# Prompt attention with the values as the stationary operand and its outputs turned back

## The reference, cut to what matters

```python
o_cmp, p_cmp = attend_dense(q, k_cmp, v_cmp, dist_c, dist_c >= 0, rel_bias)
o_sel = sel_attend(q, qpos, idx, kb, vb, rel_bias)
o_win = win_attend_prompt(q, k_win, v_win, rel_bias)
g = jax.nn.sigmoid(ngate.astype(F32)).reshape(B, T, 3, NSA_KV, NSA_REP)[..., None]
o_c = (g[:, :, 0] * o_cmp + g[:, :, 1] * o_sel + g[:, :, 2] * o_win)
```

## Time and profile before

| | |
|---|---|
| three runs | 3067.50, 3078.32, 3078.89 us |
| median | 3078.32 us |
| the profiled execution | 3082.61 us |
| its span in the trace | 3081.1 us, mean granted clock 0.944 |
| prompt attention in it, first score to last output | from 1620 to 1966 us |
| busy over the span | PE 91%, weight loads (PEld) 83%, DVE 43%, ACT 27%, POOL 13% |

### The profile page before, as it was taken

The page is one execution under the profiler, slowest core; times in us unless marked ns, Lnnn a source line. Parts: engine busy times, 40 slices in busy tenths (PEclk is TensorE's granted clock), DMA queues, the critical chain, the costliest instruction groups (busy, mean ns, idle before and its releaser), DMA issues. The chain is left out here.

```text
span 3081.1 us, 46606 instructions
## 1 busy us (share of the span) xinstructions
PE 2809.5 (91%) x17082; PEld 2572.7 (83%) x17082; DVE 1310.7 (43%) x3005; ACT 836.7 (27%) x1558; POOL 412.9 (13%) x562
## 2 busy tenths in 40 slices
PE   6999997999995799857958999899999999999998
PEld 6888997988985667753638888689989999999998
DVE  7555421443452476424526665454453332133321
ACT  4221111112011344423425665432232221011110
POOL 2121001222221233217720000000000000000000
PEclk8999998999997799978978998999999999999999
DMA  3222123223223577547731112323311113211132
GB/s 128 96 72 67 59 98 113 85 85 107 78 85 113 148 212 223 158 121 214 212 100 57 49 49 69 129 78 121 121 70 41 48 43 120 83 41 48 41 105 86
DMA packets 194205, 305.98 MB, mean 99 GB/s; under 512 B 41423, under 2 KB 147086, under 8 KB 191942
## 3 DMA queue, kind: packets, MB, share of 16 engines
q1 hardware_dynamic: 163650, 218.50, 22.5%
q0 software_dynamic: 20400, 63.59, 5.9%
q10 hardware_dynamic: 10004, 21.99, 2.1%
HBM read 238.73 MB, written 78.24 MB: 103 GB/s over the span
## 5 line engine op out<-in xcount | busy, mean ns | idle before, releaser
L2580 PE MATMUL tr_ps<-tr_act_in_r,tr_w_hi 128*128 128x364 f32 (+1 forms) x2496 | 486.2, 330 | 0.0
L2580 PEld LDWEIGHTS tr_ps<-tr_act_in_r,tr_w_hi 128*128 128x128 f32 x2496 | 428.0, 189 | 0.0
L2580 PE MATMUL tr_ps<-tr_wide_r,tr_w_hi 128*128 128x364 f32 (+1 forms) x1632 | 317.1, 330 | 0.0
L2580 PE MATMUL tr_ps<-tr_act_in_r,tr_w_r 128*128 128x364 f32 (+1 forms) x1248 | 277.7, 331 | 14.2 <-DVE tr_act_in_r L2821 7.1
L2580 PEld LDWEIGHTS tr_ps<-tr_wide_r,tr_w_hi 128*128 128x128 f32 x1632 | 278.6, 188 | 0.0
L2580 PEld LDWEIGHTS tr_ps<-tr_act_in_r,tr_w_r 128*128 128x128 f32 x1248 | 218.7, 189 | 15.5 <-issue 15.5
L63 PE MATMUL hg_ps<-tokens_hi,hg_gw_r 128*128 128x364 f32 (+1 forms) x576 | 195.7, 340 | 27.5 <-POOL hg_gw_r L2180 18.7
L65 PE MATMUL hg_ps<-tokens_hi,hg_gw_hi 128*128 128x364 f32 (+1 forms) x576 | 191.7, 333 | 0.0
L64 PE MATMUL hg_ps<-tokens_r,hg_gw_hi 128*128 128x364 f32 (+1 forms) x576 | 191.4, 332 | 0.0
L2580 PE MATMUL tr_ps<-tr_wide_r,tr_w_r 128*128 128x364 f32 (+1 forms) x816 | 180.6, 330 | 3.3 <-DVE tr_wide_r L2776 3.3
L2672 ACT ACTIVATE tr_w_hi<-tr_w 128x1024 fp32r<-128x1024 f32 (+2 forms) x76 | 88.7, 1167 | 310.0 <-DMA tr_w<-w_down_in 184.7
(11 more groups left out here) (510 smaller groups left out, 5271.3 us busy)
## 6 DMA issues: line engine op xcount, KB each, us to landing
cc_pages<-cache_in SPq DMA_DIRECT2D x256, 128.0 KB, 3.4
tr_w<-w_gate_up_in SPq DMA_DIRECT2D x44, 512.0 KB, 3.5
sa_v_pages<-cache_in POOLq DMA_DIRECT2D x256, 64.0 KB, 2.4
sa_k_pages<-cache_in SPq DMA_DIRECT2D x256, 64.0 KB, 2.3
proj_feat<-hg_g_stage POOLq DMA_DIRECT2D x24, 544.0 KB
tr_act_in<-proj_feat SPq DMA_DIRECT2D x24, 544.0 KB, 5.6
hg_gw<-w_gates_in SPq DMA_DIRECT2D x24, 512.0 KB, 3.4
tr_w<-w_down_in SPq DMA_DIRECT2D x16, 704.0 KB, 4.0
```

The lines of the kernel that those rows point to most:

```text
L2580: last = pe.matmul(ps[:, 3 * bs + c, 0:z - a], wp, xp[:, k, a:z], start=(k == 0 and n == 0), stop=(k == len(tiles) - 1 and n == 2))
```

## The change

`values` makes the values the stationary operand (64 columns) and the turned probabilities the moving one (128 columns). The selected product is written to partitions 0 to 63 of bank 7, the window product to partitions 64 to 127, key tile by key tile in turn; the compressed one is computed twice, once for each half, into the next 128 columns. All products of a tile wait for the tile's last copy. The outputs now have the head's dimensions on the partitions, so DVE copies 256 columns of bank 7 to SBUF (`take_outputs`) and PE turns them back by two transposes into the other half of bank 7 (`turn_back`): one of 128x128 and one of 64 rows. `turn_back(n - 2)` stands between the selected and the window scores of tile n. DVE's order becomes: copy and outputs of tile n - 2, then the bias of tile n. `cols` gets a third set of columns, since sums live one tile longer.

```diff
-        cols = sb("cols", [P, 2, 24])
+        cols = sb("cols", [P, 3, 24])
+        o_t = sb("o_t", [P, 2, 2 * P])
...
                 last.then_inc(S["sel_mm"], 1)
+                if n >= 2:
+                    turn_back(n - 2)
                 w0 = win_first(i) * P
...
-                def copied(x):
-
-                    if x % 4 == 0:
-                        pe.wait_ge(S["pt_copied"], base_chunk[n] + x // 4 + 1)
-
+                w0 = win_first(i)
+                heads = slice(g * HD, (g + 1) * HD)
+                sel, win = ps[0:HD, 7, 0:P], ps[HD:P, 7, 0:P]
+
+                pe.wait_ge(S["pt_copied"], base_chunk[n + 1])
                 for k in range(i + 1):
-                    copied(k)
-                    pe.matmul(ps[:, 7, 0:HD], p_all(n, k, P), v_all[:, 0, k, g * HD:(g + 1) * HD], start=(k == 0), stop=(k == i))
-                w0 = win_first(i)
-                for k in range(w0, i + 1):
-                    copied(i + 1 + k - w0)
-                    pe.matmul(ps[:, 7, HD:2 * HD], p_all(n, i + 1 + k - w0, P), v_all[:, 1, k, g * HD:(g + 1) * HD], start=(k == w0), stop=(k == i))
-                copied(len(tiles) - 1)
-                pe.matmul(ps[:, 7, 2 * HD:3 * HD], p_all(n, len(tiles) - 1, NB), vc[:, g * HD:(g + 1) * HD], start=True, stop=True).then_inc(S["o_mm"], 1)
+                    pe.matmul(sel, v_all[:, 0, k, heads], p_all(n, k, P), start=(k == 0), stop=(k == i))
+                    if w0 + k <= i:
+                        pe.matmul(win, v_all[:, 1, w0 + k, heads], p_all(n, i + 1 + k, P), start=(k == 0), stop=(w0 + k == i))
+                for x in range(2):
+                    last = pe.matmul(ps[x * HD:(x + 1) * HD, 7, P:2 * P], vc[:, heads], p_all(n, len(tiles) - 1, NB), start=True, stop=True)
+                last.then_inc(S["o_mm"], 1)
+
+            def turn_back(n):
+
+                pe.wait_ge(S["o_read"], n + 1)
+                pe.transpose(ps[:, 7, 2 * P:3 * P], o_t[:, n % 2, 0:P], ident[:])
+                pe.transpose(ps[:, 7, 3 * P:3 * P + HD], o_t[0:HD, n % 2, P:2 * P], ident[0:HD, 0:HD]).then_inc(S["o_back"], 1)
...
+            turn_back(NH * NT - 2)
             values(NH * NT - 1)
+            turn_back(NH * NT - 1)
...
+            def take_outputs(n):
+                dve.wait_ge(S["exp_done"], 3 * (n + 1))
+                dve.wait_ge(S["o_mm"], n + 1)
+                if n >= 2:
+                    dve.wait_ge(S["o_back"], n - 1)
+                dve.tensor_copy(o_t[:, n % 2], ps[:, 7, 0:2 * P]).then_inc(S["o_read"], 1)
+
             def finish(n):
...
-                dve.wait_ge(S["o_mm"], n + 1)
+                dve.wait_ge(S["o_back"], n + 1)
...
                 for n in range(h * NT, (h + 1) * NT):
+                    if n >= 2:
+                        take_outputs(n - 2)
+                        finish(n - 2)
                     bias_and_max(n)
-                    if n >= 1:
-                        finish(n - 1)
                     if n % NT == NT // 2 + 1 and h + 1 < NH:
                         queries_lo(h + 1)
-            finish(NH * NT - 1)
+            for n in range(NH * NT - 2, NH * NT):
+                take_outputs(n)
+                finish(n)
```

More of the change, by code:

```diff
@@ L1776, in prompt_attention_stage @@
         S = {n: new_sem("pa_" + n) for n in
-             ("keys_in values_in gates_in gate_exp sel_mm win_mm sel_neg win_neg exp_done pt_tr pt_copied o_mm o_read tile_set passed anyc k_zero k_hi k_split q_hi q_split").split()}
+             ("keys_in values_in gates_in gate_exp sel_mm win_mm sel_neg win_neg exp_done pt_tr pt_copied o_mm o_read o_back tile_set passed anyc k_zero k_hi k_split q_hi q_split").split()}
         out_stored = [new_sem(f"pa_out_stored{n}") for n in range(2)]
@@ L1958, in _ @@
                     nw = hi - win_first(i) * P
-                    c = cols[:, n % 2]
+                    c = cols[:, n % 3]
                     if n >= 1:
@@ L2028, in bias_and_max @@
                 dve.tensor_scalar(c[:, 1:3], c[:, 18:20], -1.0, None, ALU.mult).then_inc(S["win_neg"], 1)
+            def take_outputs(n):
[4 more added lines that the diff above has]
+                dve.tensor_copy(o_t[:, n % 2], ps[:, 7, 0:2 * P]).then_inc(S["o_read"], 1)
             def finish(n):
                 h, i = at(n)
-                c = cols[:, n % 2]
-                dve.wait_ge(S["exp_done"], 3 * (n + 1))
+                c = cols[:, n % 3]
                 dve.reciprocal(c[:, 12:15], c[:, 4:7])
@@ L2042, in finish @@
                 o = out[:, h % 2, i]
-                dve.tensor_scalar(o, ps[:, 7, 0:HD], c[:, 13:14], None, ALU.mult)
+                dve.tensor_scalar(o, ps[:, 7, 2 * P:2 * P + HD], c[:, 13:14], None, ALU.mult)
                 dve.drain()
-                dve.scalar_tensor_tensor(out=o, in0=ps[:, 7, HD:2 * HD], scalar=c[:, 14:15], in1=o, op0=ALU.mult, op1=ALU.add)
+                dve.scalar_tensor_tensor(out=o, in0=ps[:, 7, 2 * P + HD:3 * P], scalar=c[:, 14:15], in1=o, op0=ALU.mult, op1=ALU.add)
                 dve.drain()
-                dve.scalar_tensor_tensor(out=o, in0=ps[:, 7, 2 * HD:3 * HD], scalar=c[:, 12:13], in1=o, op0=ALU.mult, op1=ALU.add).then_inc(S["tile_set"], 1)
+                dve.scalar_tensor_tensor(out=o, in0=ps[:, 7, 3 * P:3 * P + HD], scalar=c[:, 12:13], in1=o, op0=ALU.mult, op1=ALU.add).then_inc(S["tile_set"], 1)
             for h in range(NH):
                 for n in range(h * NT, (h + 1) * NT):
+                    if n >= 2:
+                        take_outputs(n - 2)
+                        finish(n - 2)
                     bias_and_max(n)
-                    if n >= 1:
-                        finish(n - 1)
                     if n % NT == NT // 2 + 1 and h + 1 < NH:
                         queries_lo(h + 1)
-            finish(NH * NT - 1)
+            for n in range(NH * NT - 2, NH * NT):
+                take_outputs(n)
+                finish(n)
 LB_FLOOR = 1e-30
```

## The result

The changed kernel takes 3101.91 us, the median of five runs (3095.88 to 3108.52), against 3078.32 before: 23.6 us or 0.8% slower; the ratio of the means is 1.0083 with a 95% interval of 1.0060 to 1.0106. The forecast was 3120, the range 3085 to 3150. The profiled execution took 3101.91 us, its span is 3100.4, 19.3 more than the 3081.1 of the profiled one before.

What follows compares the result with a forecast made beforehand. PE, 91% busy, was taken to bound the kernel, the stage counting in full. +4.1 us a head, 29 for seven, +1 first head, +1 end, +11 clock make +42 on the profiled 3082.6; against the median, 3120 us, range 3085 to 3150.

Steps and rivals of the forecast that it cites:

- (a): Selected and window products on PE: paired halves at 0.055 us an instruction instead of 0.111, gaining 6.75 us a head.
- rival that the halves do not run side by side: Products on PE: at 0.110 us each they gain nothing, 12.6 us a head lost, 3180 us; chance 0.02.
- (b): Before each tile's products: PE waits for the last copy of probabilities, not the first, losing 5.46 us a head.
- rival that PE's saved time counts: Products and copies: the copy wait costs nothing, so -2.75 us a head, 3056 us; chance 0.08.
- (c): Between selected and window scores: two more turning transposes on PE cost 0.5 us a step, 4.0 a head.
- (d): Before the turning transposes: PE waits for DVE's copy of the products, mainly in small steps, 1.2 us a head.
- rival of a nearly free turning: Turning transposes at 0.2 us a step and half the wait for DVE's copy: +7 us, 3085 us; chance 0.14.
- (e): DVE's loop in step 1, the shortest: copy and turning lengthen it past PE's own way, 0.2 us a head.
- The first head: Stage's first head, partly at the low clock, where the products gain more: forecast at +1 us.
- The end: Behind the stage's last tile, copy and turning stand bare: forecast at +1 us.
- (f): Granted clock at step 1, longer with less work: falls in four heads instead of two, +11 us.
- rival of a fall in every head: Granted clock: falls in five more heads at 7.0 us each, +66 us in all, 3144 us; chance 0.15.

Runs made afterwards that it cites:

- wait alone: Kernel before with its old products, each tile's products waiting for the tile's last copy, nothing else changed; 3133.94 us, 1.0192.
- 128 rows: Changed kernel with the second turning transpose over all 128 rows and columns instead of 64 rows; 3080.35 us, 1.0002 of the kernel before.
- second record: A kernel profiled again unchanged: the kernel before took 3078.18 us, the changed kernel 3104.87 us.
- no turning: Changed kernel without DVE's copy and both turning transposes, outputs reading unturned products; 3069.14 us, 0.9978 of the kernel before.
- both repairs: Changed kernel with products in chunk order, each chunk awaiting its own copy, and the compressed product in its old form; 3042.10 us, 0.9873 of before.
- old compressed form: Changed kernel with compressed probabilities stationary again, one turning transpose and a DVE copy of 128 columns; 3073.13 us, 0.9984 of the kernel before.
- one half after the other: Changed kernel with all selected products of a tile first, then all window products; 3136.18 us, 1.0199 of the kernel before.
- order of chunks: Changed kernel with selected and window tiles laid out in turn, each chunk's products waiting only for its own copy; 3085.61 us, 1.0011 of before.

## Why the prediction was right, and where not

**(a) Products**, -6.75 forecast, -6.69 measured. The spacing in the sample attention's rows carried over. The rival that the halves do not run side by side fell.

**(b) The wait for the last copy**, 5.46 forecast, 5.42 in the changed kernel and 5.5 with the wait alone. The list of waits has 55 us, inside the forecast 50 to 80. The rival that PE's saved time counts fell with it.

**(c) and (d) Turning**, 5.2 together, 5.10 measured. From the first turning transpose to the window scores PE takes 0.26 + 0.20 = 0.46 us in steps 0 to 3 and 0.40 to 0.43 in the others, in place of 0.5: 3.5 a head, which leaves 1.6 for the wait. The one part was 0.5 too high and the other 0.4 too low; that they cancel is luck. The rival of a nearly free turning (0.2 a step) describes the variant with 128 rows better than the change: its two transposes take 0.14 to 0.19.

**(e)** 0.2 forecast, 0.21 measured, 0.14 of it in step 1; that step is 3.73, forecast 3.6 to 3.8.

So seven heads at full clock cost 28.5 us (six differences that add up to 13.6, 10.9 of the lost clock of before added to them, and 4.0 for the last head), forecast 29.

**The first head**, forecast +1, measured 52.30 - 46.77 = +5.5: it loses the 4.0 of any head, and 1.5 more (52.30 - 44.31 = 8.0 over a head at full clock, before 6.5), with a low clock at its beginning that lasted 36.1 us of it instead of 25.5. Why it lasted longer is open; in the second record of the kernel before it was 18.3 us, in that of the changed one 35.7.

**The end**, forecast +1: the last head and what stands behind it grew by 6.1, 4.0 of which is the head, so 2.1.

**(f) The clock** is the step that failed. It said that four heads would fall instead of two, because step 1 gets longer with less work in it: +11. In the profiled execution no head fell, which gave 10.9 us back. The second record, with two falls costing 3.6 + 1.3 = 4.9 us, makes the gain smaller but not the forecast right: before, the falls in heads 2 to 8 cost 10.9 and, in its second record, 6.9 + 3.9 + 3.8 = 14.6. Nor do the executions without a trace: the changed kernel's five have a higher mean clock than the 48 of before (0.948 against 0.944 to 0.945). The premise had come true: PE idles 0.86 to 1.15 us in every step of head 4, 0 to 0.72 before, so that more idle time stands beside fewer falls. In step 1 its share is the same, 0.93 of 3.73 us against 0.72 of 2.90. The place was right: all falls of all records of heads 2 to 8, but for those of the wait alone, begin 8.5 to 10.9 us after a head's start, in step 1 or at the beginning of step 2. The reason was not. Falls in heads 2 to 8 (not counting the end of the stage, where every record has one), by the length of steps 0 and 1 of head 4, one number for each record:

| kernel | steps 0 and 1, us | falls |
|---|---|---|
| before | 5.62, 2.90 | 2, 3 |
| wait alone | 6.79, 2.90 | 6, in 5 heads |
| no turning | 5.64, 3.19 | 1 |
| both repairs | 5.12, 3.38 | 0 |
| old compressed form | 5.98, 3.39 | 0 |
| 128 rows | 6.24, 3.64 | 1, of 3.4 us |
| changed | 6.53, 3.73 | 0, 2 |
| one half after the other | 7.24, 3.74 | 1 |
| order of chunks | 5.55, 3.74 | 5, 5 |

A step 1 of 3.74 us stands beside five falls and beside none. What decides is left open, and with one or two records for each kernel the rows can only rule out a strict order: neither the length of step 1, nor the wait (most falls with the old products, few with the new), nor the form of the products (the chunk order has the new form and five falls) orders the rows. The rival of a fall in every head is wrong all the same, and so is the one that transposes hold no clock.

The sum: 28.5 + 5.5 + 2.1 - 10.9 = +25.2 in the stage. It started 8.4 us earlier than in the profile of before (1611.8 against 1620.2); in the other records it starts between 1609.9 and 1619.7, the kernel before at 1617.3, so this is the stages ahead, which the change does not touch. Behind the stage 2.5 us were added. 25.2 - 8.4 + 2.5 = 19.3, the spans' difference; the profiled execution of before lay 4.3 over its median, which makes the 23.6 of the medians. The forecast's sum was 42, so it was 18 too high: 21.9 too much for the clock, 5.9 for what lies outside the stage and 0.5 for seven heads, less 4.5 and 1.1 too little for the first head and the end, and less those 4.3. In part these cancel by chance; the range holds without any term for the clock too (3120 - 11 = 3109).

## What to carry to other kernels

A product that becomes cheaper only counts if what feeds it is early enough: an order that makes all products wait for the last copy gave 5.4 of 6.7 us back, and using the chunks as they come kept 5.0 of these. A transposed result has to be turned back, and the form of the turning matters more than its size: a transpose with another number of rows between full ones cost 2.1 us a head more than one twice its size. Where the clock falls at some places only, a forecast from one record should give it a wide term of both signs: of these kernels some had fewer falls than before and some more.

## What was not expected of the hardware

A transpose of 64 rows between full instructions is dearer than one of 128: the turning pair takes 0.40 to 0.46 us from start to start against 0.14 to 0.19. The Trainium skill, TensorEngine Tiling (Array Packing), section Key Properties, says that a change of the tiling mode drains the engine; the trace agrees in the later starts, the draining itself it does not show. What the two changes of a turning cost here is 2.1 us in eight steps, about 0.27 a step.

PE starts products out of the program's order when they belong to the other half: the first window instruction starts at 1773.22, ahead of three selected ones that precede it (1773.33 the first of them). The Trainium skill, TensorE: Matmul & The Clock Gate, Part 3, section The mechanism, says that matmuls start and end in program order; the starts in this trace do not agree.

The same kernel can show the same five falls of the clock, in the same heads and of the same lengths, in two executions, when the kernels beside it change theirs from one execution to the next. That does not make it every execution's: with the chunk order three of ten ran 8 us and more below the other seven, at a higher mean clock (0.945 against 0.935 to 0.942).
